# Row tiles of 32 tokens by 4 picks, h2 copied across partitions by TensorE and ScalarE, and a PSUM ring of 5 tiles

## What is computed

```python
h2 = _rmsnorm(x, norm_g[1]) * (1 + sc2) + sh2
# _peer, for a block of tokens xt = h2:
qp = (xt @ wq).reshape(t, 8, 2, 128)
sc = einsum('thsk,hsnk->thsn', qp, subkeys)         
top_s, top_i = top_k(sc, 16)
cand_s = top_s[:, :, 0, :, None] + top_s[:, :, 1, None, :]
best_s, best_p = top_k(cand_s, 16)
expert = take(top_i[0] * 128 + top_i[1], best_p)    
g = softmax(best_s)
act = gelu(einsum('thkd,td->thk', u_tab[expert], xt))
out = einsum('thk,thkd->td', g * act, v_tab[expert])
y = final_norm(x + gt2 * out)
```

## Time and profile before

| what | us |
|---|---|
| median of 3 runs (lowest, highest) | 4936.25 (4924.78, 4938.27) |
| the profiled execution, its own time | 4929.44 |
| its span | 4927.7 |
| PE / DVE / ACT / POOL busy | 3968.5 / 2747.1 / 1593.8 / 1616.5 |
| DMA moved | 1687 MB, of which gathers 1342 MB |

### The profile page before, as it was taken

One profiled execution on the slowest core, in us unless ns is written; L12 is line 12 of the kernel. 1 busy time (PEld: TensorE's weight loads), 2 busy tenths in 40 slices (PEclk: granted clock), 3 DMA queues, 4 the chain that ended last, 5 costly groups with the idle time before them and its releaser, 6 DMA issues. The chain is left out here.

```text
span 4927.7 us, 44934 instructions
## 1 busy us (share of the span) xinstructions
PE 3968.5 (81%) x12301; PEld 1584.9 (32%) x12301; DVE 2747.1 (56%) x6701; ACT 1593.8 (32%) x4955; POOL 1616.5 (33%) x1312
## 2 busy tenths in 40 slices
PE   6999898999999865999876658988876755666666
PEld 4644355554434321344321213343322210111110
DVE  1112678433234499455569895545468996544544
ACT  4111244332122243323333333323343333333333
POOL 0000123221122232343333334344333334555554
PEclk8999999999999975999987769999977766666666
DMA  6644787878798987999999899999999878999998
GB/s 252 223 182 176 252 314 290 302 268 333 283 367 342 340 346 272 375 380 380 393 369 351 363 358 369 422 396 384 412 418 370 341 294 347 409 421 415 415 422 354
DMA packets 290059, 1687.33 MB, mean 342 GB/s; under 512 B 29136, under 2 KB 71184, under 8 KB 111120
## 3 DMA queue, kind: packets, MB, share of 16 engines
q0 software_dynamic: 184320, 1342.26, 68.8%
q1 hardware_dynamic: 97472, 318.79, 17.0%
q10 hardware_dynamic: 8016, 23.42, 1.5%
HBM read 1646.57 MB, written 37.78 MB: 342 GB/s over the span
## 5 line engine op out<-in xcount | busy, mean ns | idle before, releaser
L913 POOL DMA_INDIRECT slots<-in_peer,idxR x1280 | 1610.2, 1258 | 3257.8 <-PE ps L1178 2525.8
L1178 PE MATMUL ps<-slots,lhs 128*64 128x512 f32 x5120 | 1667.9, 765 | 818.3 <-ACT lhs L958 815.9
L1447 DVE CUSTOM_DVE_ANT_0 slots<-slots,h2R 128x1024 f32<-128x1024 f32 x1280 | 1540.2, 1224 | 814.8 <-issue 730.1
L1166 PE MATMUL ps<-ring,arena 128*128 128x512 f32 (+1 forms) x3996 | 1591.0, 553 | 28.8 <-DMA ring<-in_wq 22.2
L1166 PEld LDWEIGHTS ps<-ring,arena 128*128 128x128 f32 x3996 | 760.6, 195 | 884.2 <-issue 830.2
L1178 PEld LDWEIGHTS ps<-slots,lhs 128*64 128x64 f32 x5120 | 330.8, 158 | 2018.6 <-ACT lhs L958 1695.3
L953 ACT ACTIVATE gelus<-dots 128x1 f32<-128x1 f32 x1280 | 256.0, 200 | 1596.4 <-DVE dots L1447 1593.8
L958 ACT ACTIVATE lhs<-fold,wgts 128x64 f32<-128x64 f32 x1280 | 445.1, 348 | 41.9
L954 ACT ACTIVATE wgts<-gelus,gsmR 128x1 f32<-128x1 f32 x1280 | 377.1, 295 | 42.1
L1166 PE MATMUL ps<-ring,slots 128*128 128x512 f32 (+1 forms) x704 | 250.9, 518 | 0.4 <-DMA ring<-in_wz 0.4
L1166 PEld LDWEIGHTS ps<-ring,slots 128*128 128x128 f32 x704 | 134.0, 191 | 114.3 <-issue 105.9
(11 more groups left out here) (194 smaller groups left out, 2340.4 us busy)
## 6 DMA issues: line engine op xcount, KB each, us to landing
ring<-in_whead SPq DMA_DIRECT2D x24, 2048.0 KB, 9.4
ring<-in_wa SPq DMA_DIRECT2D x24, 2048.0 KB, 9.6
ring<-in_wq SPq DMA_DIRECT2D x16, 2048.0 KB, 18.4
slots<-in_peer,idxR POOLq DMA_INDIRECT x1280, 11.4
ring<-in_wlate SPq DMA_DIRECT2D x16, 1024.0 KB, 7.5
ring<-in_wgc SPq DMA_DIRECT2D x16, 1024.0 KB, 9.4
ring<-in_wgb SPq DMA_DIRECT2D x8, 2048.0 KB, 10.0
ring<-in_wout SPq DMA_DIRECT2D x8, 2048.0 KB, 12.6
```

The source lines that it names most:

```text
L913: g.indirect_dma_start(out=slot(R), out_offset=None, in_=a["peer"], in_offset=bass.IndirectOffsetOnAxis(ap=idxR[:, p % KEEP, g2, col:col + ...
L1166: done = mm(out, lhsT, rhs, start=n == 0, stop=n == len(pairs) - 1)
L1178: done = mm(ps[j * HALF:(j + 1) * HALF, g2, :], lhs[:, R % LHS, :], slot(R)[:, D + j * UW:D + (j + 1) * UW], start=start, stop=stop)
L1447: v.tensor_tensor_reduce(out=u, in0=u, in1=h2R[:, g2, :], scale=1.0, scalar=0.0, op0=ALU.mult, op1=ALU.add, accum_out=dots[:, R % LHS:R % ...
```

## The change

- A row is a tile of 32 tokens by 4 picks. The folding matrix is 128 x 32, and a row takes four matmuls of 32 output partitions by 256 columns. The sums of 32 tokens (a quarter of a chunk) take 256 columns of a bank.
- Rows of a chunk go by halves: in 64 rows the quarters 0 and 1 alternate by 8 rows and all four pairs pass (16 rows a pair), then the quarters 2 and 3. There are four `ev` a chunk.
- h2 of a chunk is read once (`ldh`, 512 KB into h2in). For each quarter, two `rep` events follow: TensorE copies its 32 tokens to the four groups of partitions by selecting columns of the identity, into bank 2, and ScalarE copies that to h2R.
- topc and softmax write to `vals` in one instruction per head each; `mv` (TensorE, 16 matmuls of 16 columns) carries indices and weights to the row tiles' partitions, ScalarE copies the weights to gsmR, and `mw` (VectorE) copies the indices to idxR. A pair counts as ready after `mw`.
- The ring of front tiles has 5 banks, and every mv takes a tile of it.
- starts[k] of groups of three goes by pair 2, and a part of a ranking is planned at 2.8 us.

```diff
-BANKS = 6
+QT = P // 4
+PICKS = TOP // 4
+BANKS = 5
 def row_of(R):
-    p, rr = divmod(R, ROWS)
-    pair, g, qq = rr // 32, rr // 16 % 2, rr % 16
-    return p, g, pair, pair * 16 + qq, 2 * pair + qq // 8
+    p, n = divmod(R, ROWS)
+    g, pair = 2 * (n // HALF) + n // 8 % 2, n // 16 % 4
+    return p, g, pair, 8 * pair + n % 8, 2 * pair + n // PICKS % 2
@@ Plan.ranking
             for hd in range(2):
                 for part in "abc":
-                    ev = self.add("top" + part, ..., dve=3.3)
-                    if part == "c" and hd == 0 and m:
-                        before, ib = divmod(m - 1, n)
-                        ev.ready = (BASE[k] + ib, before)
+                    self.add("top" + part, ..., dve=2.8)
                     yield
+                    if m and hd == 0 and part == "c":
+                        self.moved(k, m - 1)
+                        yield
+                    if m and hd == 1 and part == "a":
+                        self.laid(k, m - 1)
+                        yield
+    def moved(self, k, m):
+        self.at["mv", z] = self.add("mv", 1, g=k, p=BASE[k] + i, j=pair, z=z, pe=1.6, act=.3).t
+    def laid(self, k, m):
+        ev = self.add("mw", g=k, p=BASE[k] + i, j=pair, z=z, y=self.at["mv", z], dve=.3)
+        ev.ready = (BASE[k] + i, pair)
@@ Plan.merge
-        starts = [self.ready[BASE[k], int(len(cs) > 2)] ...
+        starts = [self.ready[BASE[k], 2 * (len(cs) > 2)] ...
@@ Plan.spare: one ldh a chunk, and two rep a quarter once its predecessor in h2R is used up
+                if (p, g) not in self.loaded and p in self.loaded and ... (
+                        h2_load(p, g) == 1 or rows >= last_row(*self.quarter_before(p, g)) + 2):
+                    self.events += [Event("rep", p=p, c=ORDER[p], j=g, h=half) for half in range(2)]
@@ scalar
+                elif k == "rep":
+                    if h2_load(ev.p, ev.j) > 1 and ev.h == 0:
+                        eng.wait_ge(s["dot_done"], last_row(*plan.quarter_before(ev.p, ev.j)) + 1)
+                    eng.wait_ge(s["rep_done"], copied(ev) + 1)
+                    A_(h2R[:, ev.j % 2, ev.h * UW:(ev.h + 1) * UW], ps[:, 2, :], ACT.Copy).then_inc(s["h2R_done"], 1)
+                elif k == "mv":
+                    filled(eng, t)
+                    ...
+                    A_(gsmR[:, ev.p % KEEP, :, 8 * ev.j:8 * ev.j + 8], moved(t)[:, :, 1, :],
+                       ACT.Copy).then_inc(s["gsm_done"], 1)
@@ tensor, row
-                for j in range(2):
-                    done = mm(ps[j * HALF:(j + 1) * HALF, g2, :], lhs[:, R % LHS, :],
-                              slot(R)[:, D + j * UW:D + (j + 1) * UW], start=start, stop=stop)
+                for j in range(4):
+                    done = mm(sums(g2)[j * QT:(j + 1) * QT, :], lhs[:, R % LHS, :],
+                              slot(R)[:, D + j * GW:D + (j + 1) * GW], start=start, stop=stop)
@@ tensor
+                if k == "rep":
+                    pe.wait_ge(s["h2_in"], 16 * (ev.p + 1))
+                    if copied(ev):
+                        pe.wait_ge(s["h2R_done"], copied(ev))
+                    for i in range(4):
+                        done = mm(ps[i * QT:(i + 1) * QT, 2, :], ident[:, ev.j * QT:(ev.j + 1) * QT],
+                                  h2in[:, ev.h * UW:(ev.h + 1) * UW], start=True, stop=True)
+                    done.then_inc(s["rep_done"], 1)
+                elif k == "mv":
+                    room(t)
+                    pe.wait_ge(s["val_done"], ev.z + 1)
+                    for g2 in range(4):
+                        for i in range(4):
+                            done = mm(bank(t)[i * QT:(i + 1) * QT, 4 * g2 * PICKS:4 * (g2 + 1) * PICKS],
+                                      ident[:, g2 * QT:(g2 + 1) * QT], vals[...], start=True, stop=True)
@@ vector, topc
-                for g2 in range(2):
-                    for i in range(2):
-                        done = v.scalar_tensor_tensor(out=idxR[...], ...)
+                if ev.z >= 2:
+                    filled(dve, at["mv", ev.z - 2])
+                st.step(v.scalar_tensor_tensor(out=vals[:, ev.z % 2, :, 0, ev.j, :], ...))
@@ vector
+                elif k == "mw":
+                    dve.wait_ge(s["gsm_done"], ev.z + 1)
+                    ...
+                    st.link(v.tensor_copy(idxR[...], moved(ev.y)[:, :, 0, :]))
+                    dve.sem_inc(s["idx_done"], 1)
+                    dve.sem_inc(freed[ev.y % BANKS], 1)
```

More of the change, by code:

```diff
@@ L386, in ranking @@
                 for part in "abc":
-                    ev = self.add("top" + part, g=k, i=m, h=2 * pair + hd, j=hd, c=cs[i], p=BASE[k] + i,
-                                  z=4 * BASE[k] + m, y=self.at["rank", k, m],
-                                  act=.8 * (hd == 0 and part == "c"), dve=3.3)
-                    if part == "c" and hd == 0 and m:
-                        before, ib = divmod(m - 1, n)
-                        ev.ready = (BASE[k] + ib, before)
-                    yield
-        ev = self.add("gsm", g=k, z=4 * BASE[k] + pairs - 1, act=.8, dve=2.0)
-        ev.ready = (BASE[k] + n - 1, 3)
-        yield
+                    self.add("top" + part, g=k, i=m, h=2 * pair + hd, j=hd, c=cs[i], p=BASE[k] + i,
+                             z=4 * BASE[k] + m, y=self.at["rank", k, m],
+                             act=.8 * (hd == 0 and part == "c"), dve=2.8)
+                    yield
+                    if m and hd == 0 and part == "c":
[4 more added lines that the diff above has]
+                        yield
+        self.add("gsm", g=k, z=4 * BASE[k] + pairs - 1, act=.8, dve=1.0)
+        self.moved(k, pairs - 1)
+        self.laid(k, pairs - 1)
+        yield
+    def moved(self, k, m):
+        pair, i = divmod(m, len(GROUPS[k]))
+        z = 4 * BASE[k] + m
+        self.at["mv", z] = self.add("mv", 1, g=k, p=BASE[k] + i, j=pair, z=z, pe=1.6, act=.3).t
+    def laid(self, k, m):
+        pair, i = divmod(m, len(GROUPS[k]))
+        z = 4 * BASE[k] + m
+        ev = self.add("mw", g=k, p=BASE[k] + i, j=pair, z=z, y=self.at["mv", z], dve=.3)
+        ev.ready = (BASE[k] + i, pair)
     def make_front(self):
@@ L434, in merge @@
         wall = [max(ev.cost) for ev in self.front]
-        starts = [self.ready[BASE[k], int(len(cs) > 2)] for k, cs in enumerate(GROUPS)] + [len(self.front)]
+        starts = [self.ready[BASE[k], 2 * (len(cs) > 2)] for k, cs in enumerate(GROUPS)] + [len(self.front)]
         due = [0.0] * (len(self.front) + 1)
@@ L882, in _ @@
                                     base=0, pattern=[[-1, P]], channel_multiplier=1))
[L883 to L886, removed]
+            for b in range(4):
+                st.link(g.affine_select(out=fold[:, :], in_=fold[:, :], compare_op=ALU.not_equal, fill=1.0,
+                                        base=-QT * b, pattern=[[-1, QT]], channel_multiplier=1))
             for b in range(4):
@@ L903, in _ @@
             for R in range(NR):
-                p, g2, pair, col, head = row_of(R)
+                p, g2, pair, col, _ = row_of(R)
                 if R == 0:
@@ L908, in _ @@
                 if R == plan.few:
-                    pool.wait_ge(s["idx_done"], 8 * BASE[1])
-                pool.wait_ge(s["idx_done"], 2 * pair_number(p, pair) + head % 2 + 1)
+                    pool.wait_ge(s["idx_done"], 4 * BASE[1])
+                pool.wait_ge(s["idx_done"], pair_number(p, pair) + 1)
                 if plan.displaced(R) >= 0:
@@ L1207, in _ @@
                                       start=kk % 2 == 0, stop=kk % 2 == 1)
+                    done.then_inc(full[t % BANKS], 1)
+                elif k == "mv":
+                    room(t)
+                    pe.wait_ge(s["val_done"], ev.z + 1)
+                    for g2 in range(4):
+                        for i in range(4):
+                            done = mm(bank(t)[i * QT:(i + 1) * QT, 4 * g2 * PICKS:4 * (g2 + 1) * PICKS],
+                                      ident[:, g2 * QT:(g2 + 1) * QT],
+                                      vals[:, ev.z % 2, i, :, :, :].rearrange("p v h s -> p (v h s)"),
+                                      start=True, stop=True)
                     done.then_inc(full[t % BANKS], 1)
```

126 lines of the change are left out of this document (65 added, 61 removed).

## The result

| what | before | after |
|---|---|---|
| median of 4 runs each on one chip, us | 4930.51 (4924.35 to 4938.27) | 5070.83 (5070.27 to 5079.79) |
| ratio, 95% interval | | 1.0288 [1.0266, 1.0310] |
| the profiled execution / its span, us | 4929.44 / 4927.7 | 5070.93 / 5069.2 |
| PE / DVE / ACT / POOL busy, us | 3968.5 / 2747.1 / 1593.8 / 1616.5 | 3480.9 / 2703.1 / 1596.9 / 1413.0 |
| DMA moved, MB | 1687 | 1683 |

The change makes the kernel slower by 2.9%. TensorE's busy time fell by 488 us, and the time rose by 141: the work removed was not what the end hung on. I forecast 4962 with a range to 5060; the sign was right, the size was not, and the result lies 11 us above the range.

The account below looks back on a forecast made before the run. It took stretches as bound by TensorE (heads 2 and 3, pooling with group 1, group 2), VectorE (rankings) or DMA (group 3, tail). Terms 5 + 77 - 43 + 17 - 67 - 32 + 20 + 0 + 59 = +36 gave 4965, taken 4962; range 4845 to 5060.

Parts of the forecast that it names:

- The size of a row on TensorE: TensorE, per row: 0.43, or 0.48 with switching, against 0.95 now; 0.45 us saved where TensorE is the bound.
- Rival D: Row tiles on TensorE: four column groups don't overlap with each row's own weights; about 5060 us, chance 0.04.
- The planner term: Heads: rows held back, then bursts of 3, 16 and 34 rows; heads 559 against 490, with clock +77 us.
- Start: +5: Before the heads: one move and its wait cost +5 us; the rest hides under the hT reload.
- Group 2: Group 2: rows 150 x 0.93 become 124 x 0.5, rep +11; -67 us, stretch near 470.
- Pooling and group 1: Pooling with group 1: 126 rows x 0.43 = -54, four quarters of rep +11; -43 us.
- Group 3: Group 3, taken as DMA-bound: 8 more rows x 2.5 = +20 us.
- Rival C: Group 3: little TensorE work lets the clock fall to 1.2 GHz, +53; about 5015 us, chance 0.06.
- Tail: Row-only tail: 26 rows x 2.51 = +65, h2 read once -6; from row 935, near 885 us.
- Rival B: Rankings: mv waits 4 us on VectorE in all 32 z, +96; about 5055 us, chance 0.12.
- The move itself: TensorE: 40 moves of 32 tiny instructions, 1.7 to 4.2 us each, taken as 2.5.
- Rival A: Heads and rankings: mv, exps, laid and first landings find other work ahead; 4834 to 4880 us, chance 0.27.

Follow-up runs that it names:

- run 1: Kernel before with only rows 16, 32 and 48 of chunk 0 held until the changed order has their index: 5021.46 us, 1.0173.
- run 4: Changed kernel with the first four h2 copies put behind the fourth query instead of ahead of the queries: 5069.36 us, 1.0272.
- run 7: Changed kernel with the row order of before, four quarters in h2R, and the final norm's gain left out: 4966.56 us, 1.0082.
- the fastest kernel: Run 11's kernel with LAST_PACE 2.6 instead of 2.9, putting more of group 3's rows beside the front: 4849.00 us, 0.9845.
- run 6: Changed kernel with h2 brought by DMA, each quarter read four times, and no rep on TensorE and ScalarE: 5034.85 us, 1.0212.
- run 10: Changed kernel with mv and mw one step of the ranking later and nothing else: 5022.21 us, 1.0194.
- run 9: Run 7's kernel with mv and mw one step of the ranking later, the final norm's gain again left out: 4912.01 us, 0.9963.
- run 11: Run 8's kernel, the whole computation, with mv one step later: 4857.46 us, 0.9861.
- run 3: Changed kernel with group 0's rows starting only where pair 3 of chunk 0 is ready, so none is held: 5026.48 us, 1.0183.
- run 5: Kernel before with rows of groups of three falling due from pair 2 instead of pair 1: 4951.26 us, 1.0036.
- Run 8: Changed kernel, whole computation, with the row order of before, h2 by DMA, starts by pair 1 and a ring of six: 4928.18 us, 0.9996.

## Why the prediction was right in sign and short in size

**What held.** The size of a row on TensorE: kernel after shows 0.64 for one and 1.07 for two at full clock, 0.43 each more, as worked out from L1206; rows in pooling and group 1 cost 73.5 us for 129.6, -56 (forecast -54). Rival D fell with that. The planner term was the right mechanism and the right size: bursts of 16 and 37 rows (16 and 34), heads 578 us (559, and 8 for the clock), head 2 196 (191), the tile behind the burst 8.81 for 7.17, and run 1 gave +87 for the holds by themselves. The last ranking ends at row 928 (935), the tail takes 896 (885). In the heads mv's waits average 3.3 us (23.1 over 7), the figure taken.

**What failed.** Stretch by stretch the measured length less the forecast is: start +28, heads +11, pooling and group 1 +17, ranking 1 -13, group 2 +42, ranking 2 -20, group 3 +12, ranking 3 +14, tail +14; together +105. Two steps of the sum failed by more than their size. At the start, four copies of h2 had no term at all, and the overlap ("the rest hides under the hT reload") isn't there. In group 2 the saving of the new rows was taken in full, for fewer rows than ran there.
- "Start: +5 (one move and its wait ahead of the last queries; the rest hides under the hT reload)": it took +33. TensorE comes to the same matmuls of the plan (ahead of the queries) at 488.71 before and 504.68 after:

```profile
488.71 1.97 PE L1368 MATMUL ps<-ident,tmp 128*128 128x128 f32 x8 [0.68 <-DVE tmp L1740]
```

```profile
494.61 1.94 PE L1246 MATMUL ps<-h2in,ident 128*32 128x512 f32 x8 [5.53 <-DMA h2in<-h_scratch]
...
504.68 1.97 PE L1438 MATMUL ps<-ident,tmp 128*128 128x128 f32 x8
```

  One us of these 16 was there before; the other 15 are the load of h2 and chunk 0's four copies. The first move and its wait add 4. The reload of hT (what the heads' first tiles read; SP's queue) and the first gathers (POOL) in the two timelines, first before, then after:

```profile
559.58 11.69 SPq L755 DMA_DIRECT2D arena<-hT_scratch  x8
```

```profile
525.52 1.16 POOL L913 DMA_INDIRECT slots<-in_peer,idxR  x1 [490.05 <-DVE idxR L1500]
```

```profile
579.59 27.02 SPq L798 DMA_DIRECT2D arena<-hT_scratch  x8
```

```profile
578.97 1.16 POOL L955 DMA_INDIRECT slots<-in_peer,idxR  x1 [543.25 <-DVEq L1813]
...
585.48 1.80 POOL L955 DMA_INDIRECT slots<-in_peer,idxR  x1 [0.31 <-issue]
```

```profile
575.87 3.62 PE L1467 MATMUL ps<-arena 128*128 128x128 f32 x16
612.52 9.65 PE L1217 MATMUL ps<-arena,ring 128*128 128x512 f32 x16 [33.03 <-DMA arena<-hT_scratch]
```

  The reload begins 0.1 us after TensorE's last work on the queries (579.49), so what lies ahead of that pushes it: it begins 20 us later. I took its start as fixed. And it lasts 33 us to the first tile, not 20 (559.6 to 579.6): before, the first six gathers had been issued at 525, long before it; now they start with it, six times 1 MB, 15 us at 405 GB/s, and the stretch 580 to 612 above shows the DMA full. 20 + 13 = 33. Runs 4 and 7 and the fastest kernel keep this wait (33.5, 32.8, 33.8 us). A start without the collision was not tried. How much of the +28 is left at the end isn't shown either: run 4 takes 10 us out of the start, and the whole is 1.5 us shorter.
- Group 2: -25, not -67, the largest miss, and the sign "group 2 near 470" did not come (513). 138 rows ran there for 148 before, not 124 for 150. Rows kept TensorE busy for 79.6 us after 143.1, so 64 us less and not 78; the copies of h2 took 10.5 busy and 7.4 waiting, 18 for my 11; TensorE's other waits rose from 23 to 33 us and the tiles took 5 us more. The DMA's share was 0.96 before and is 0.95 after, at 379 GB/s both times: I had called this stretch bound by TensorE alone.
- The rows missing from ranking 2 (119 for my 134) are those, and it is 20 us better than forecast for it. Ranking 1 is 13 better: POOL waited six times for an index there, 129.3 us, but the 40 us of first landings that I charged don't show in its length. The three stretches sum to -73 for -82; that this is so near is luck.
- Pooling and group 1: -26, not -43. Rows gave what was forecast; the copies of h2 took 10.1 busy and 7.7 waiting, 18 for my 11 (their second halves waited for ScalarE, 3.6 us at most). The other 10 us are not assigned.
- Group 3: +32 for +20 (its 215 rows as forecast; the 12 us over are not assigned). The copies of h2 had no term here; they took 20.4 busy and 22.5 waiting, but run 6 without them is only 3 us shorter from z 27 to z 28. Rival C fell: the clock is 0.91 here, but the DMA share is still 0.96.
- Ranking 3: +14 for 0. TensorE idles 134.9 us before 12 moves there, in a stretch where VectorE is busy for 405 of 479; by the landmarks of run 10, moving mv takes 19 us off it.
- Tail +73 for +59: seven rows more than forecast, 17 us.
- The heads, +88 for +77: three rows more in the burst, 7 us; the rest is not assigned.

Rival B (mv's waits 3 us dearer in all 32 z of the rankings, the whole about 5055) is near the measured time and did not happen: the rankings are together 19 us shorter than forecast, which is what the 15 rows missing from ranking 2 make. What its mechanism costs in full isn't shown, since 260 us of idle time before mv remain in run 10; what one step later gives in the rankings is 22 us in run 10 and nothing in runs 9 and 11.

The move itself was over-priced: 32 instructions take 0.63 us (0.44 at full clock), not 2.5. The Trainium skill, TensorEngine Tiling (Array Packing), Instruction Overhead, gives about 60 cycles each, by which a move is an estimated 0.8 us; the trace is nearer to that than to my rows, and a little below it. The sum holds seven moves in the heads and one at the start; 1.9 us less for each would make the forecast 15 us lower still, and so the miss larger.

How the 141 divide can be bounded and not summed: holds 87 and starts 21, put into the kernel before; mv's place 49 and copies of h2 36, taken out of the kernel after; 193 in all, less what the tiles save. They overlap: runs 3 and 5 show that a front made faster gives time back in a later, DMA-bound part. Run 8, at 0.9996, says that the tiles of 32 x 4 save no more than mv in its first place, the late start and the added reads of h2 cost; run 11, that with mv late the same kernel is 71 us faster.

**Where the chances stood wrong.** Rival A, "the hand-overs hide", had 0.27 and fell at every point: first landings, waits and copies all show. On the slow side stood B, C and D with 0.22 in all, each priced alone, and none of them was what happened. Holds, waits, copies and the start all add in the same direction, and the range should have reached to their sum.

## What to carry to other kernels

A change of tile shape that also changes the order of the tiles moves the point at which each index is first needed: write out the planned list and look for work held back, since the gathers missing from a TensorE-bound stretch were paid for later here (run 1 gave none of its 87 us back). A hand-over that crosses engines (VectorE to TensorE to VectorE) is put one step of other work behind its producer. Don't rank waits by their total: moving mv gained most in the heads, where 23 to 36 us of idle time stood before it, and little in the rankings, where it was some 380 and VectorE is the bound. Judge the new tiles only when both are settled: here the same tiles gave 1.029, and 0.985 with mv late and the row order, h2 reads, ring and starts of before.

## What the runs showed of the hardware

- Matmuls of 128x32 weights by 16 columns took 14 ns each (32 in 0.44 us, changed kernel at 939.75) at a granted clock of 1.00 and 20 ns (32 in 0.63 us, run 7 at 911.91) at 0.50, their weights loaded in the same time; my sum had 78 ns.
- A direct reload of 4 MB took 20 us to the first tile alone (kernel before), and 33 together with six gathers of 1 MB (the changed kernel).
- In DMA-bound stretches TensorE's rows took 1.08 us each where one takes 0.64 at full clock (granted clock 0.53 on the mean of the tail, the lower level being 1.2 GHz; before 0.65), and it cost nothing: rows came about 2.5 us apart. TensorE's busy time over the span (3480.9) so understates by how much the work shrank.
